# Key/value and query projections of a two-block network, rewritten as Strassen steps

## The reference, cut to what matters

```
h   = _rms(x, g) * (1.0 + scale) + shift
kvf = h @ kv_w                                   # k, v: 1024 columns each
k   = _head_rms(k, k_norm_g)                     # rms over each head's 64 columns
F   = cumsum(log_sigmoid(f_logit + f_bias))      # forget gate, 16 columns
q, z = split(h2 @ w_in, 2)                       # q, z: 1024 columns each
q   = _head_rms(q, q_norm_g) * HEAD_DIM ** -0.5
o   = attention(q, k, v, F) * silu(z)
```

## Time and profile before

| | |
|---|---|
| median of 3 runs | 4815.03 us (4814.56 to 4815.03) |
| the profiled execution's own time | 4818.94 us |
| its span | 4817.2 us |
| TensorE matmul busy | 4442.0 us, 92% |
| TensorE weight load busy | 2849.5 us, 59% |
| VectorE busy | 1483.5 us, 31% |
| ScalarE busy | 976.4 us, 20% |
| GpSimd busy | 268.8 us, 6% |

### The profile page before, as it was taken

The page is one execution under the profiler, slowest core; times in us unless marked ns, Lnnn a source line. Parts: engine busy times, 40 slices in busy tenths (PEclk is TensorE's granted clock), DMA queues, the critical chain, the costliest instruction groups (busy, mean ns, idle before and its releaser), DMA issues. The chain is left out here.

```text
span 4817.2 us, 60007 instructions
## 1 busy us (share of the span) xinstructions
PE 4442.0 (92%) x24520; PEld 2849.5 (59%) x24520; DVE 1483.5 (31%) x3904; ACT 976.4 (20%) x2108; POOL 268.8 (6%) x349
## 2 busy tenths in 40 slices
PE   7996999999999998997899999979889995999996
PEld 3443444444565544653788888864456653888885
DVE  5407331101684223844211111121235534111111
ACT  2011122111564103732100000021025531000001
POOL 0100000000220000000001000000000000000000
PEclk9998999999999998998999999989999997999998
DMA  7567201222320102114577777741150011888887
GB/s 276 219 113 305 88 18 54 81 77 83 127 106 9 67 34 92 34 45 166 214 259 254 265 251 258 254 156 57 51 163 19 19 45 71 310 315 318 315 313 255
DMA packets 123191, 741.20 MB, mean 154 GB/s; under 512 B 13456, under 2 KB 47504, under 8 KB 87552
## 3 DMA queue, kind: packets, MB, share of 16 engines
q1 hardware_dynamic: 96256, 654.83, 37.3%
q0 software_dynamic: 25840, 83.12, 5.9%
q10 hardware_dynamic: 912, 0.76, 0.0%
HBM read 653.75 MB, written 85.43 MB: 153 GB/s over the span
## 5 line engine op out<-in xcount | busy, mean ns | idle before, releaser
L367 PE MATMUL psum<-w_ring,arena 128*128 128x512 f32 (+3 forms) x2760 | 1127.5, 568 | 24.6 <-PEq L162 18.7
L2253 PEld LDWEIGHTS psum<-arena,w_ring 128*128 128x128 f32 x8192 | 1022.1, 192 | 15.9 <-issue 15.9
L2253 PE MATMUL psum<-arena,w_ring 128*128 128x160 f32 (+1 forms) x8192 | 1026.5, 288 | 4.6 <-ACT arena L2335 3.1
L367 PEld LDWEIGHTS psum<-w_ring,arena 128*128 128x128 f32 x2760 | 526.5, 193 | 579.4 <-issue 532.4
L367 PE MATMUL psum<-arena,w_ring 128*128 128x512 f32 (+1 forms) x1648 | 707.4, 586 | 2.8 <-DVE arena L300 1.7
L367 PEld LDWEIGHTS psum<-arena,w_ring 128*128 128x128 f32 x1648 | 310.2, 191 | 365.0 <-issue 360.9
L2268 PE MATMUL psum<-w_ring,arena 128*128 128x512 f32 x1024 | 450.0, 592 | 0.0
L2394 DVE TENSOR_TENSOR arena<-arena,psum 128x320 f32<-128x320 f32 (+1 forms) x128 | 58.2, 454 | 957.1 <-PE psum L2253 957.1
L1378 PE MATMUL psum<-arena 64*128 64x256 f32 (+5 forms) x1056 | 319.5, 526 | 33.3 <-PEq L162 31.4
L2319 ACT ACTIVATE arena<-psum 128x320 f32<-128x320 f32 (+1 forms) x128 | 52.5, 410 | 1310.8 <-PE psum L2253 1310.8
L2268 PEld LDWEIGHTS psum<-w_ring,arena 128*128 128x128 f32 x1024 | 189.7, 190 | 214.9 <-issue 214.9
(11 more groups left out here) (353 smaller groups left out, 2947.5 us busy)
## 6 DMA issues: line engine op xcount, KB each, us to landing
w_ring<-in_wstream SPq DMA_DIRECT2D x264, 2048.0 KB, 7.8
x_rows<-arena SPq DMA_DIRECT2D x18, 512.0 KB, 2.6
xn_rows<-arena POOLq DMA_DIRECT2D x18, 512.0 KB, 2.9
arena<-x_rows SPq DMA_DIRECT2D x9, 1024.0 KB, 9.0
arena<-f_rows SPq DMA_DIRECT2D x8, 1024.0 KB, 7.6
arena<-in_x_first SPq DMA_DIRECT2D x4, 1024.0 KB, 21.8
u_T<-arena POOLq DMA_DIRECT2D x16, 256.0 KB, 2.7
z_T<-arena POOLq DMA_DIRECT2D x16, 256.0 KB, 2.9
```

The costliest lines, as they stand in the source:

```text
L367: last = cr.nc.tensor.matmul(bank_ap, l, r, start=(k == 0), stop=(k == len(pairs) - 1))
L2253: last = nc.tensor.matmul(half(bank0 + v)[:, c], w[:, k, m * P:(m + 1) * P], xT[:, k, :], start=(k == 0), stop=(k == KT - 1))
```

## The change

`block_heads` now works in 16 steps n of a 256-row by 512-column result: token blocks q and q + 4 (q = n mod 4) by one weight tile (t = n div 4). Each is split into 2x2 quarters of 128 rows, 512 inner and 256 columns, and computed by seven products in place of eight, each 4 matmuls of 256 columns. The products add up in PSUM where they can (`a`, `b`, `c`: three 256-column pieces in two banks), and ScalarE copies `a` out between two of them. The steps are interlaced on TensorE: products 1 and 2 of step n (`pe_open`), 7 of n - 1 (`pe_third`), 5 and 6 of n (`pe_second`), 4 and 3 of n - 1 (`pe_close`). VectorE adds the pieces in `raw` or `stage` (`dve_11`, `dve_22`, `dve_12`), makes the sums of quarters of the input (`quad_sums`, four operations of 512) and of each weight tile (`w_sums_12`, `w_sums_34`, four operations of 1024). The weight sums live in the third ring slot, so the ring has two slots here; the input sums live where `Xr` was, so `Xr` is stored to DRAM in `block_a_out` and loaded again in the attention.

All row stores now stand on SyncE, GpSimd has none, and ScalarE issues the weight loads and two of the head loads. The forget gate's chain stands at step 9 on VectorE and its sums ahead of step 10 on TensorE. The eight scalings stand in twos around `dve_22` in steps 9 and 10. For z, ScalarE applies Silu in four operations of 256 columns, three of them after the sums. `N` is 16; `turns(n, j)` is the j-th turn of step n: three in each of steps 11 to 15, one in step 16.

```diff
-SLOT = [FIRST_SLOTS.get(n) if n < W_MOD1 else (2, 0, 1)[(n - W_MOD1) % RING] for n in range(N_TILES)]
+def slot_of(n):
+    if n < W_MOD1:
+        return FIRST_SLOTS.get(n)
+    if n < W_KV:
+        return (2, 0, 1)[(n - W_MOD1) % RING]
+    if n < W_EIN:
+        return (1, 0)[(n - W_KV) % 2]
+    return (2, 1, 0)[(n - W_EIN) % RING]
+SLOT = [slot_of(n) for n in range(N_TILES)]
...
+    def a(self, n):
+        return self.cr.bank[2 + 2 * (n % 2)][:, 0:256]
+    def b(self, n):
+        return self.cr.bank[3 + 2 * (n % 2)][:, 0:256]
+    def c(self, n):
+        return self.cr.bank[3 + 2 * (n % 2)][:, 256:512]
...
+    def pe_open(self, pe, n, of):
+        if n >= 2:
+            pe.wait_ge(self.made21, n - 1)
+        self.run(self.a(n), of(1), True).then_inc(self.opened, 1)
+        if n >= 2:
+            pe.wait_ge(self.made12, n - 1)
+        self.run(self.b(n), of(2), True).then_inc(self.first, 1)
+    def pe_second(self, pe, n, of):
+        pe.wait_ge(self.made11, n + 1)
+        self.run(self.c(n), of(5), False)
+        pe.wait_ge(self.kept1, n + 1)
+        self.run(self.a(n), of(6), False).then_inc(self.second, 1)
+    def pe_third(self, pe, n, of):
+        pe.wait_ge(self.kept2, n + 1)
+        self.run(self.a(n), of(7), False).then_inc(self.third, 1)
+    def pe_close(self, pe, n, of):
+        pe.wait_ge(self.kept3, n + 1)
+        self.run(self.a(n), of(4), False).then_inc(self.fourth, 1)
+        pe.wait_ge(self.made22, n + 1)
+        self.run(self.c(n), of(3), False).then_inc(self.fifth, 1)
+    def act_1(self, act, n, to):
+        act.wait_ge(self.opened, n + 1)
+        self.cr.nc.scalar.activation(to, self.a(n), ACT.Copy).then_inc(self.kept1, 1)
...
+    def dve_11(self, dve, n, to):
+        dve.wait_ge(self.kept1, n + 1)
+        dve.wait_ge(self.first, n + 1)
+        self.cr.nc.vector.tensor_tensor(to, to, self.b(n), ALU.add).then_inc(self.made11, 1)
...
+SUM_OF = {5: 0, 6: 1, 7: 2, 3: 3}
+def token_part(h, S, p, k, a, n):
+    if p in SUM_OF:
+        v = S[:, a:a + n, SUM_OF[p], k]
+        return v if n > 1 else v[:, 0]
+    kk, i = {1: (k, a), 2: (4 + k, a), 4: (4 + k, a + 4)}[p]
+    return h[:, kk, i * P:(i + n) * P]
+def weight_part(w, T, t, p, k):
+    return {1: w[:, k, 0:256], 2: w[:, 4 + k, 0:256], 3: w[:, 4 + k, 256:512], 7: w[:, k, 256:512],
+            5: T[:, 0, k], 6: T[:, 1, k], 4: T[:, 2 + t % 2, k]}[p]
+def quad_sums(cr, ln, h, S, i):
+    tt = cr.nc.vector.tensor_tensor
+    at = lambda k, j: h[:, k:k + 4, j * P:(j + 1) * P]
+    ln(tt(S[:, i, 0], at(0, i + 4), at(4, i + 4), ALU.add))
+    ln(tt(S[:, i, 1], S[:, i, 0], at(0, i), ALU.subtract))
+    tt(S[:, i, 2], at(0, i), at(0, i + 4), ALU.subtract)
+    return tt(S[:, i, 3], at(4, i), S[:, i, 1], ALU.subtract)
...
+            for i in range(NT):
+                sp.wait_ge(fol.fin, i + 1)
+                sp.dma_start(xa_d[i * P:(i + 1) * P, :], Xr[:, i]).then_inc(xs[i // 2], 16)
             sp.wait_ge(un.full, 32)
-            for t in range(2):
-                cr.load_w(sp, W_AOUT + t + RING)
+            cr.load_w(sp, cr.next_tile(W_AOUT + 1))
+            for q in range(4):
+                sp.wait_ge(xs[q], 32)
...
+                if i >= 6:
+                    fol.placed(dve, i - 2)
+                    dve.wait_ge(xs[i - 6], 32)
+                    ln(quad_sums(cr, ln, hkv, x_sums(cr), i - 6))
...
+            def store_rows(n):
+                t, q = n // 4 - 2, n % 4
+                qd.whole(sp, n)
+                if z_T:
+                    sp.wait_ge(silu, n - 7)
...
+            for n in range(9, N + 1):
+                for v in TURN.get(n, ()):
+                    store_t(v)
+                store_rows(n - 1)
+                if n == 11 and forget:
                     sp.wait_ge(f_row, 1)
                     sp.dma_start(F_d, FT[0:HB]).then_inc(f_st, 16)
             for k in range(2):
                 sp.wait_ge(kst_[k], 16 * 8)
+                sp.wait_ge(st[k], 32 * 4)
+            cr.load_w(sp, w0 + 5)
+            if z_T:
+                cr.load_w(sp, W_EIN)
...
+                if n == 10 and forget:
                     pe.wait_ge(f_ls, 1)
...
+                if n < N:
+                    if n % 4 == 0:
+                        cr.wait_w(pe, w0 + n // 4)
+                    qd.pe_open(pe, n, factors(n))
+                for v in turns(n, 0):
+                    turn(v)
+                if n:
+                    if n % 4 == 1:
+                        pe.wait_ge(w_sum, 2 * (n // 4) + 2)
+                    qd.pe_third(pe, n - 1, factors(n - 1))
+                for v in turns(n, 1):
+                    turn(v)
+                if n < N:
+                    if n % 4 == 0:
+                        pe.wait_ge(w_sum, 2 * (n // 4) + 1)
+                    if n in sums:
+                        pe.wait_ge(x_sum, sums.index(n) + 1)
+                    qd.pe_second(pe, n, factors(n))
+                for v in turns(n, 2):
+                    turn(v)
+                if n:
+                    qd.pe_close(pe, n - 1, factors(n - 1))
...
+            for n in range(N + 1):
+                m = n - 1
+                if n < N:
+                    if n >= 10:
+                        act.wait_ge(st[n % 2], 32 * ((n - 8) // 2))
+                    if n == 9:
+                        act.wait_ge(red, 16)
+                    qd.act_1(act, n, blocks(n)[0])
+                if n:
+                    qd.act_3(act, m, blocks(m)[3])
+                if n < N:
+                    qd.act_2(act, n, blocks(n)[1])
...
+                if m >= 8:
+                    qd.act_21(act, m, blocks(m)[2], rows_func)
+                    if z_T:
+                        act.wait_ge(qd.made11, m + 1)
+                        nc.scalar.activation(blocks(m)[0], blocks(m)[0], rows_func)
+                        act.wait_ge(qd.made22, m + 1)
+                        nc.scalar.activation(blocks(m)[3], blocks(m)[3], rows_func)
+                        act.wait_ge(qd.made12, m + 1)
+                        nc.scalar.activation(blocks(m)[1], blocks(m)[1], rows_func).then_inc(silu, 1)
...
+                if n in (4, 8, 12):
+                    act.wait_ge(qd.fifth, n)
+                    cr.load_w(act, w0 + n // 4 + 1)
+                if n == 13 and ahead:
+                    for k in range(2):
+                        act.wait_ge(kst_[k], 16)
+                        act.wait_ge(st[k], 32)
+                    for to, of in ahead[1]:
+                        act.dma_start(to, of).then_inc(nxt, 16)
+                if n == 8:
+                    act.wait_ge(var, 1)
+                    nc.scalar.activation(hs[:, 2], hs[:, 1], ACT.Sqrt).then_inc(std, 1)
...
+            def w_sums_12(t):
+                w = cr.w(w0 + t)
+                cr.wait_w(dve, w0 + t)
+                if t:
+                    dve.wait_ge(qd.second, 4 * t)
+                ln(tt(T[:, 0], w[:, 0:4, 256:512], w[:, 0:4, 0:256], ALU.subtract))
+                tt(T[:, 1], w[:, 4:8, 256:512], T[:, 0], ALU.subtract).then_inc(w_sum, 1)
+            def w_sums_34(t):
+                w = cr.w(w0 + t)
+                ln(tt(w[:, 0:4, 256:512], w[:, 4:8, 256:512], w[:, 0:4, 256:512], ALU.subtract))
+                dve.wait_ge(w_sum, 2 * t + 1)
+                if t >= 2:
+                    dve.wait_ge(qd.fourth, 4 * (t - 1))
+                tt(T[:, 2 + t % 2], w[:, 4:8, 0:256], T[:, 1], ALU.subtract).then_inc(w_sum, 1)
...
+            for n in range(N + 1):
+                m = n - 1
+                if n < N:
+                    if n % 4 == 0:
+                        w_sums_12(n // 4)
+                    qd.dve_11(dve, n, blocks(n)[0])
+                    if n % 4 == 0:
+                        w_sums_34(n // 4)
+                for v in turns(n, 0):
+                    place(v)
+                if n == 9:
+                    dve.wait_ge(std, 1)
+                    nc.vector.reciprocal(hs[:, 3], hs[:, 2]).then_inc(rst, 1)
+                    dve.wait_ge(rst, 1)
+                if n in (9, 10):
+                    scale_rows(4 * (n - 9), 4 * (n - 9) + 2)
+                if n:
+                    qd.dve_22(dve, m, blocks(m)[3])
+                if n in (9, 10):
+                    scale_rows(4 * (n - 9) + 2, 4 * (n - 9) + 4)
+                for v in turns(n, 1) + turns(n, 2):
+                    place(v)
+                if n:
+                    qd.dve_12(dve, m, blocks(m)[1])
+                if 2 <= n <= 8:
+                    reduce(m - 1)
...
+                if n == 9 and forget:
                     dve.wait_ge(f_l, 1)
...
+                if then is not None and 13 <= n <= 15:
+                    dve.wait_ge(qd.fifth, n)
+                    ln(quad_sums(cr, ln, then, S, n - 13))
...
-    attention(cr, "fox", steps, lambda p: fox_loads(cr, p), 1, [], s_buf, t_buf, r_buf, cr.small[:, 380:764], gate=gate, own=own)
```

(1 more changed line is left out.)

## The result

The changed kernel takes 4784.86 us (median, 4780.92 to 4789.64), beside 4815.03 us before: a ratio of 0.9938, interval 0.9921 to 0.9955. That is 30 us faster, where 47 were forecast, and above the range's 4781.

What follows compares the result with a forecast made beforehand. TensorE, busy 92% of the span, was taken as the bound. Savings of 52.2 us, less waits, plus 0.5 at the end, gave 46.9: 4818.9 to 4772.0 us profiled, 4768 as median, range 4761 to 4781.

Steps and rivals of the forecast that it cites:

- Weight loads from ScalarE come whole steps ahead of use: In both blocks' steps, weight loads issued by ScalarE were claimed to be early enough; no cost was entered.
- Rival 1: Larger give-backs in the blocks through lowered clock, late stores, slow sums or visible weight loads: 4773 to 4783; chance 0.25.
- A step: TensorE's 28 matmuls per step take 12.11 us against 13.74 for two units before, saving 52.2 us over both blocks.
- 2 us are gained: Bound on TensorE's step cost: if records run at the 512-column rate, 2 us more are saved; not taken.
- the simple form: Skill's record time, columns over clock plus 2.5 ns; claimed to fit 216 ns at 256 columns within 1 ns.
- Step 0 and the last: TensorE waits at each block's ends for lack of covering products: 0.85 us in step 0, 0.8 in the last.
- Step 10 of `block_kv`: TensorE stands 2.6 us ahead of the running sums, waiting for the chain behind `dve_12` of step 8.
- Step 9: Late reductions, Sqrt and, in `block_kv`, a table load make TensorE wait 0.5 us there, 0.05 in `block_bq`.
- Step 10 of `block_bq`: `act_1` waits for step 8's half of `stage` to be stored, making TensorE 0.35 us late; 0.3 taken.
- `w_sums` at steps 4, 8 and 12: VectorE's weight sums finish at 5.1 us against 5.19: no cost, no margin; 3 us if a quarter slower.
- The attention: Behind `block_bq`, one more weight tile delays pair 1's loads, GpSimd 0.5 us late with 2 us left: no cost.
- Rival 2: In the attention, pair 1's loads end up to 13 us later if `Xr` loads alongside: 4770 to 4778; chance 0.05.

Runs made afterwards that it cites:

- e1: Changed kernel with ScalarE issuing step 12's weight load behind its first copy of step 13, both head loads behind that of step 14; 4761.57 us.
- e4: Changed kernel with step 12's weight load issued by SyncE directly behind the row stores, head loads left in place; 4769.2 us.
- e9: Changed kernel with ScalarE issuing the weight load once product 1 of step 13 is done, head loads behind `act_1` of step 14; 4774.57 us.
- e10: e5 with the weight load put ahead of another row store, at the end of ScalarE's step 14; 4777.34 us.
- e6: Changed kernel with half the weight load left ahead of the store, half behind `act_1` of step 13, head loads as in e1; 4771.04 us.
- e5: e1 with the forget gate's running sums, their copies and their store also one step later; 4759.87 us.
- e0: The changed kernel measured again without any edit, beside e9 and e10 on one chip; 4783.81 us.

## Why the prediction was wrong

**The step that failed** is the sentence "Weight loads from ScalarE come whole steps ahead of use", by which these loads were costed at nothing. It asked when the load's own data is wanted, and not what is issued right behind it. What a 2 MB load delays here is the store behind it, until it has landed itself; `stage` has two halves, and the reader of step 13 needs the half back some 4.5 us after the store goes out (931.46 - 4.09 - 922.86). e1 removes 4.4 us of `block_kv` and 12.4 of `block_bq` by moving the issue alone (6.0 of `block_kv`, but for the 1.66 us of clock that e1 lost behind the 2.25 us wait), e4 and e9 show that order decides, e10 that the step does not matter. Measured in the changed kernel: 12.1 us of waits and 5.7 of clock, against 0. Rival 1 had "some 3 from stores landing late", a sixth of it, and with no mechanism behind it: I had taken 2.6 us for the landing, which is a median.

The trace of the kernel before held the case already, in the stores that the median hides. There SyncE issues a 2 MB load:

```profile
931.76 0.34 SPq L168 DMA_DIRECT2D w_ring<-in_wstream  x1
```

GpSimd's next row store is issued at 932.66 and SyncE's next store of turned rows at 932.99. These two by line, with the us to their landing:

```profile
v_rows<-arena POOLq DMA_DIRECT2D x1, 256.0 KB, 8.0
k_T<-arena SPq DMA_DIRECT2D x1, 256.0 KB, 8.1
```

One of them stands on another queue than the load, one on the same, and both are late. In `block_bq` it is the same behind the load of 1168.48 (7.9 and 8.0 us). It cost nothing there: ScalarE wrote that half of `stage` again only at 946.38, 13.7 us behind the store's issue, where step 13 now leaves 4.5.

The Trainium skill names half of this. "DMA: Bandwidth & Descriptors", section "Issuing engines are not separate DMA queues", says that transfers started by different engines end up on the same 16 DMA engines and interleave. The trace agrees that a queue of one's own protects no one. Its section "Queues, rings and completion order" has each DMA engine take turns between the queues, and drain a whole packet of "≈9-17 descriptors typical" before the turn passes. The profile has 144 records for the 2 MB load, which would be 9 for each of the 16 engines that the page gives. If a record is a descriptor, then by the page a whole load can be one packet on each engine, and a store behind it waits for all of it; that is an estimate from the page. The rows agree with the outcome (landings 0.7 us behind the load's in e6, `act_1` 1 us behind it in the changed kernel), but they do not name the DMA engine of a record, so the mechanism is not shown.

**The other terms held.**
- A step: `dve_12` to `dve_12` at 853.35 and 865.43, 12.08 us (forecast 12.11). The main term was 52.2 us. e5, without the waits behind the loads and the one of 2.25 us, has blocks of 429.8 us, 51.3 under the 481.1 of before. (The bound "2 us are gained" at the rate of 512 columns is 2.8 by its own figures. The 216 ns of a record fit the simple form that the prediction cites only with the time of the columns taken twice, as it writes it; taken once, the form gives 109 ns. So the agreement "within 1 ns" is weaker than it reads, and the row decides.)
- Step 0 and the last: 0.68 and 0.47 us (0.85 and 0.8). Step 10 of `block_kv`: 2.25 (2.6). Step 9 shows no wait (0.5): the table load and Sqrt end at 869.3, but `dve_11` comes at 869.64 and TensorE still has product 7 to do. Step 10 of `block_bq`: none (0.3). The sum had 5.9 us of give-backs, less the turns' waits of 0.50 us that go in each block. Counted in the same way, the rows give 2 x (0.68 + 0.47) + 2.25 - 1.0 = 3.6, so it was 2.3 over-sized. The clock behind the wait of 2.25 us, for which the sum had nothing, takes 1.7 of that back in e1. e1's blocks are 48.2 us under before, against 46.9; so apart from the failed step the sum comes close partly because these two errors offset each other.
- `w_sums` at steps 4, 8 and 12: no wait in the changed kernel; at step 8 VectorE's chain ended with `dve_11` at 857.27 + 0.41, inside the 5.19 us. At step 12, e0, e5 and e10 wait 0.42, 0.30 and 0.23 us, but there `act_1` waits for the store of step 10.
- The attention: GpSimd's first use of pair 1 comes at 1224.80, 21.4 us after its first operation there at 1203.38; before, at 1256.77, 21.3 after. Rival 2 did not come about.
- The clock: rival 1's mechanism was right (a gap of 3 us costs the clock about 1.5 us, one of 4.9 us 2.6). It was hung on the gap of step 10, which cost 1.7 us in six executions of eight, and not on the larger ones behind the loads.

**What stays open.** Whole times move by up to 6.5 us more than the block spans explain (the medians of e1 and the changed kernel are 23.3 us apart, their blocks 16.8), in stretches with the same instructions. So e1 at 4761.6 us, under the forecast of 4768, confirms the blocks and not each microsecond of the whole. Why the store waits for the whole load, and is not served between its packets, no run here shows.

## What to carry to other kernels

Before a large load is moved to an engine "with time", list the small transfers that are issued while it is under way (here 0.6 to 5.7 us behind its issue), on its own queue or another, and who waits for each: each of them lands only with the load (here 8 us after its issue), and that costs time where the reader has less room. Issue it when the last such reader has passed, or right behind the store on the same queue, where the order can't slip, if what follows on that queue can wait. Look for the case in the trace before, by single transfers: a median over 16 hides the one that was late. And count a wait that reaches TensorE with its clock: here those of 2.7 us or more inside a block cost another 1.4 us to 3 us, those of 2.25 us 1.7 in six executions of eight.

## What was not expected of the hardware

- Two stores of 256 KB whose issue began 0.6 us behind a 2 MB load from another queue reached their reader just behind it, 8.6 us later, where such stores land in 2.2; behind 1 MB they landed after 6.0 us. Those whose issue had ended 0.3 us ahead of such a load's were not held up (2.4 us). Of two stores of one queue around the issue of such a load, the one issued ahead took 2.8 us, and the one whose issue ended 0.1 us behind the load's took 9.0.
- Waits of 2.24 and 2.25 us left the clock at 1.00 in two executions (the changed kernel's and e6's) and lowered it in six (0.79 in e1's window), among them that of the same changed kernel in e0; 2.01 us left it (16 records in 3.72 us behind it), 2.81 us did not (5.41).
